# Three-branch attention: VectorE's copy of the turned rows moves one step back, behind the next maximum and the reciprocal

## The reference

```python
def nsa_mixer(q, k_cmp, v_cmp, k_sel, v_sel, k_win, v_win, gate_logit, ...):
    # for each block of 128 queries and each of 16 heads
    p_c = masked_softmax(einsum(q, kc) * scale, cmp_end <= t)      # 31 compressed keys
    o_c = einsum(p_c, vc)
    p_s = masked_softmax(einsum(q, k_g) * scale, valid_s)          # selected blocks
    o_s = einsum(p_s, v_g)
    p_w = masked_softmax(einsum(q, kw) * scale, valid_w)           # window
    o_w = einsum(p_w, vw)
    return gate[0] * o_c + gate[1] * o_s + gate[2] * o_w
```

## Time and profile before

| | |
|---|---|
| time before, median of 3 runs | 1916.68 us (1914.93 to 1918.02) |
| the profiled execution's own time | 1919.38 us |
| its span, first to last instruction | 1917.6 us |
| granted PE clock, mean | 0.988 of full speed |
| PE busy in the span | 1839.3 us (96%) |
| DVE busy | 1027.5 us (54%) |
| ACT busy | 828.2 us (43%) |
| POOL busy | 592.6 us (31%) |
| the three-branch attention, scores to last turn | about 1375 to 1536 us |

### The profile page before, as it was taken

How to read it: one execution, slowest core, us unless ns; L and a number is a source line. 1 busy time by engine, 2 the same in 40 slices (tenths; PEclk the granted TensorE clock), 3 DMA queues, 4 the chain that set the end, 5 groups by cost and what they waited for, 6 DMA issues and landing times.

```text
span 1917.6 us, 27389 instructions
## 1 busy us (share of the span) xinstructions
PE 1839.3 (96%) x10554; PEld 1451.5 (76%) x10554; DVE 1027.5 (54%) x2006; ACT 828.2 (43%) x1569; POOL 592.6 (31%) x421
## 2 busy tenths in 40 slices
PE   8999999997888999999999999999999999999998
PEld 7878889842223778767888888889888888888886
DVE  3170442521111869663477676842577725767677
ACT  4123651311111543375554544353377655444543
POOL 4344431011110233356322223233055643232221
PEclk9999999999999999999999999999999999999999
DMA  7223404699999412121132223222203012233321
GB/s 236 98 94 118 140 1 154 251 392 419 420 420 370 167 45 88 46 88 35 54 132 88 88 88 120 98 94 67 45 2 89 2 44 88 88 131 108 113 88 45
DMA packets 86867, 252.06 MB, mean 131 GB/s; under 512 B 12212, under 2 KB 19700, under 8 KB 74448
## 3 DMA queue, kind: packets, MB, share of 16 engines
q1 hardware_dynamic: 81344, 238.79, 33.9%
q0 software_dynamic: 4592, 9.30, 1.3%
q10 hardware_dynamic: 800, 2.20, 0.3%
HBM read 241.89 MB, written 15.73 MB: 134 GB/s over the span
## 4 chain that ended last, share of the span: by engine, by line
PE 86%; DVE 4%; DMA 4%; ACT 3%; issue 2%; POOL 0%; ACTq 0%; DVEq 0%; POOLq 0%
PE psA L1606 42%; PE psS L2054 4%; PE psA L1649 3%; DMA ring<-in_w_down_e 3%; PE psA L2018 2%; PE psO L2352 2%; PE psO L1836 2%; PE psT L1836 2%; PE psS L1836 2%; PE psT L2402 2%; DVE x L3089 2%; DMA big<-in_w_down_e 1%; PE psA L1471 1%; PE psA L1785 1%; PE psS L1649 1%
## 5 line engine op out<-in xcount | busy, mean ns | idle before, releaser
L1290 POOL TENSOR_TENSOR w_slot<-ring,w_slot 128x1024 fp32r<-128x1024 f32 (+1 forms) x81 | 214.0, 2656 | 524.7 <-ACT w_slot L2433 524.4
L1606 PE MATMUL psA<-hT_hi,w_slot 128*128 128x512 f32 x960 | 298.2, 390 | 0.0
L2433 ACT ACTIVATE w_slot<-ring 128x1024 fp32r<-128x1024 f32 (+2 forms) x183 | 196.8, 1086 | 164.4 <-DVE ring L3089 75.0
L1606 PEld LDWEIGHTS psA<-hT_hi,w_slot 128*128 128x128 f32 x960 | 180.4, 188 | 37.3
L1606 PE MATMUL psA<-hT_lo,w_slot 128*128 128x512 f32 x480 | 187.0, 390 | 0.0
L3089 DVE TENSOR_TENSOR w_slot<-ring,w_slot 128x1024 fp32r<-128x1024 f32 x98 | 119.9, 1225 | 115.7 <-ACT w_slot L2433 115.7
L3089 DVE TENSOR_TENSOR x<-psA,x 128x512 f32<-128x512 f32 (+1 forms) x186 | 117.1, 662 | 104.2 <-PE psA L1606 68.8
L1606 PE MATMUL psA<-w_slot,hid_part 128*128 128x512 f32 x672 | 161.4, 390 | 0.0
L2433 ACT ACTIVATE big<-psA 128x512 f32<-128x512 f32 (+6 forms) x134 | 61.7, 482 | 208.7 <-PE psA L1606 126.0
L1606 PEld LDWEIGHTS psA<-w_slot,hid_part 128*128 128x128 f32 x672 | 126.2, 188 | 26.1
L2433 ACT ACTIVATE scr<-scr,stat 128x384 f32<-128x384 f32 (+3 forms) x224 | 123.7, 555 | 19.1 <-DVE stat L4079 9.8
(11 more groups left out here) (557 smaller groups left out, 4450.2 us busy)
## 6 DMA issues: line engine op xcount, KB each, us to landing
ring<-in_mlp_w SPq DMA_DIRECT2D x32, 2048.0 KB, 8.1
ring<-in_w_in SPq DMA_DIRECT2D x8, 2048.0 KB, 8.1
ring<-in_w_gate_e SPq DMA_DIRECT2D x14, 1024.0 KB, 16.3
ring<-in_w_up_e SPq DMA_DIRECT2D x14, 1024.0 KB, 20.7
ring<-in_w_down_e SPq DMA_DIRECT2D x13, 1024.0 KB, 28.3
big<-in_w_down_e SPq DMA_DIRECT2D x12, 1024.0 KB, 26.4
ring<-in_ab_w_in SPq DMA_DIRECT2D x5, 2048.0 KB, 8.6
scr<-in_w_down_e SPq DMA_DIRECT2D x7, 1024.0 KB, 27.0
```

The lines of the kernel that those rows point to most:

```text
L1290: nc.gpsimd.tensor_tensor(part(w_lo, c), raw_piece(c), part(w_hi, c).bitcast(F32), ALU.subtract)\
L1606: ins = pe.matmul(o, a, b, start=(at == 1), stop=(at == 3 * len(terms)))
L2433: return nc.scalar.activation(o, i, f, **kw)
```

## The change

DVE's loop of the three-branch attention issues the reciprocal or the weighing directly behind the maximum, and the copy behind that; and the copy at step i is that of item i - 7 instead of item i - 6. No instruction is added or removed, and the loops of the other engines are as they were.

```diff
                                 op0=ALU.add, op1=ALU.min, accum_out=negm[:, n_items + i:n_items + i + 1]).then_inc(n_masked, 1)
-                    k = i - TURN_LAG - 1
+                    if 2 <= i < n_nsa + 2 and nsa[i - 2]["g"]:
+                        weigh_nsa(i - 2)
+                    k = i - TURN_LAG - 2
                     if 0 <= k < n_nsa and k % 2:
                         dve.wait_ge(n_turned, k + 1)
                         if k >= TURNED:
                             dve.wait_ge(n_values, values_before(k - TURNED))
                         nc.vector.tensor_copy(turned_probs[k % TURNED][:, 0:nsa[k]["n"]], psT[k % 2][:, 0:nsa[k]["n"]])\
                             .then_inc(n_copied[k % 2], 1)
-                    if 2 <= i < n_nsa + 2 and nsa[i - 2]["g"]:
-                        weigh_nsa(i - 2)
```

## The result

The changed kernel takes 1933.61 us (median of 4 runs, 1933.16 to 1936.64) against 1917.35 us (median of 4, 1914.93 to 1918.14): 16.3 us more, a ratio of 1.009 with a 95% interval of 1.0073 to 1.0108. The forecast was 1929, slower; the time lies in its range, and the loss was about a third larger than the 12.5 us forecast.

A forecast was written before the change was run, and what follows sets the result against it. The prediction took PE to bound the attention, with DVE's later copies stalling its turns: 8.1 us at plain places + 6.7 at weighings - 2.1 given back = 12.7 us, in the runs' measure 1916.7 + 12.5, rounded to 1929 us; range 1920.5 to 1936.

The forecast's parts named there:

- What bounds the attention: Attention: PE sets the pace, busy 146.7 of 152.0 us; a change on DVE counts only where PE waits for it.
- the loop of the psT buffer: Turn of item k, its copy, turn of item k + 2; a maximum now delays the copy, 1.70 us against 1.36 at 384 wide.
- Where it binds: Odd items with no value block before the buffer's next turn: from item 15 on 24 plain places, plus 7 with a weighing.
- The sign that POOL's share of PE's waits would go: Changed kernel's profile: PE's waits for POOL's product, 2.1 us in nine turns before, were to go.
- The price of a plain place: Loops without value block or weighing: stalls of 0.2 to 0.34 us by width, 6.9 us, plus 1.2 for reciprocals: 8.1 us.
- With a weighing: Copies behind the 0.82 us weighing: items 11, 45, 79, 113 cost 3.9 us, items 29, 63, 97 cost 2.8.
- What is given back: PE's nine waits for POOL, 2.1 us, can go as the reciprocal comes earlier; nothing comes back behind the attention.
- The sum: Whole kernel: 8.1 + 6.7 - 2.1 = 12.7 us more, forecast as 1929 us; chance 0.72.
- No change: Rival for the psT loop: two rotating buffers hide one's copy behind the other's turn; 1916.7 us, chance 0.06.
- Faster: Rival: POOL's wait for the reciprocal is the brake in narrow tiles; 5 us less, 1911, chance 0.07.
- Slower by 5 us: Rival: PE is delayed only at the seven weighings, 6.7 us less 2.1; 1921.5 us, chance 0.13.
- The rival of the clock: New stalls in the attention lower PE's granted clock, about 1.7 us per fall, five adding 8; 1937 us, chance 0.02.

The follow-up runs named there:

- dose: Kernel before, with the first 128 columns copied once more ahead of every odd copy, a delay of 0.33 us: 1925.51 us, ratio 1.0033 to 1.0058.
- the halves: Kernel before with reciprocal and weighing ahead of the copy, 1918.23 us; kernel before with only the copy moved to item i - 7, 1930.36 us.
- reciprocal first: Kernel before, with reciprocal and weighing ahead of the copy, which stays that of item i - 6: 1918.23 us, ratio 0.9993 to 1.0012.
- weighing behind: Changed kernel, with the cmp items' weighing behind the copy again and the pairs' reciprocals in front: 1932.94 us, ratio 1.0062 to 1.0089 to before.

## Why the prediction was right, and where it was off

- *What bounds the attention, and the loop of the psT buffer.* Right, and shown from both sides: the copy behind the next maximum costs 14.1 us without the rest of the change, the rest of the change with the copy in front of that maximum costs nothing that the times show, and a measured dose costs itself less the slack at the places worked out ahead.
- *Where it binds.* Right. In the changed kernel the turn that closes the loop starts 0.14 or 0.15 us behind the end of the copy at all 31 places forecast, item 67 among them, which was put at nothing and cost 0.12 us. From item 11 on, three more turns do so that were not counted, those of items 11, 113 and 127 (0.39, 0.24 and 0.26 us); every other one comes at least 0.37 us behind its copy. The list's 29 waits are 28 of the 31 and item 11; at items 81 and 111 it names POOL, and at item 69 the wait is under PEld. Copies delayed only in the other places cost nothing that the times show. The sign that POOL's share of PE's waits would go can't be read from the list, as said above.
- *The price of a plain place.* Too small: 8.1 us forecast, 10.8 measured (the 24 loops from turn to turn, after against before). The step that failed is the 0.04 us between the end of a turn and DVE's maximum. I had read it from a copy. A maximum starts 0.15 us behind the turn (1424.47 against an end at 1424.32), also in the narrow tile (1521.20 against 1521.05). 0.11 us at 31 places are 3.4 us. With it the loop of item 37 is 0.49 + 0.15 + 0.48 + 0.55 + 0.15 = 1.82 us, what was measured. The earlier trace rows start with a copy and could not show it, but the trace of the kernel before does: each of the 14 maxima that a turn released starts 0.14 or 0.15 us behind it. One of them with its turn, and one of the first steps with its scores:

```profile
1444.60 0.60 PE L2402 MATMUL psT<-const,scr 128*128 128x128 f32 x4
...
1445.34 0.69 DVE L4079 CUSTOM_DVE_ANT_0 scr<-psS,const 128x512 f32<-128x512 f32 x1 [1.93 <-PE psT L2402]
```

```profile
1377.43 0.44 PE L2389 MATMUL psS<-nsa_k,nsa_q 128*128 128x128 f32 x2
...
1377.90 0.29 DVE L4079 CUSTOM_DVE_ANT_0 scr<-psS,const 128x128 f32<-128x128 f32 x1 [1.03 <-PE psS L2389]
```

  The second pair says that it is not the instruction itself: in the first seven steps a maximum waits for its scores alone, and the four of them that waited start 0.03 or 0.04 us behind the scores. Nor is it enough that there are two waits: the copies from item 9 on have two as well and start 0.04 us behind the turn. What makes the 0.15 stays open. At items 59, 75 and 83 the period was also shorter than I took it (1.56, 1.56 and 1.47 us, with cmp scores or, at 83, the first 384-wide scores between the turns), and they cost 0.63 to 0.69 us, not 0.27 to 0.36.
- *With a weighing.* 6.7 forecast, 7.9 measured, at the seven items named, 0.92 to 1.33 us each. At item 11 I had taken 0.6 for waits that were there anyway; it cost 1.09.
- *What is given back.* 2.1 forecast. The turns that came earlier did so by 2.0 us in all, at nine turns, mostly where PE had waited for POOL. That is about as forecast, though some of it lies inside the places above.
- *The sum.* In the profiled executions the attention grew by 18.2 us against 12.7: the 31 places cost 18.7 us, not 14.8, and the other loops together gave back 0.5. The medians grew by 16.3.
- *The rivals.* No change falls: the two buffers hide a copy only up to the slack, 0 to 0.33 us, and the rule of the Trainium skill to rotate through PSUM banks ("Perfetto Trace Analysis", section "Optimizing Tensor Performance") holds just to there. Faster falls with the halves: the reciprocals in front bring 0.7 us, and not 5. Slower by 5 us falls: the plain places cost more than the weighings. The rival of the clock falls too: the granted clock of the changed kernel's attention is 1.00, against 0.99 before; what it did is told below.

## What to carry to other kernels

When an instruction is moved back on one engine, find the buffer that it frees and write down the loop through it: producer, hand over, everything that now stands ahead of it on its engine, itself, hand over; and compare that with the time after which the producer comes back. An engine with a quarter of its time idle, as DVE here before the change (busy 112.6 of 152.0 us), can still hold the bound engine up, if its idle time lies in front of the work and not behind it. If two instructions are released by the same event, the one that frees a buffer for the bound engine goes first, and short ones that feed an engine with slack may go ahead of it only while it is waiting anyway.

## What the runs showed of the hardware

After the same stretch of waiting the granted clock of PE fell in some executions and not in others. In the execution of before, PE was busy 2.14 of the 4 us ahead of 1390, and the granted clock of the next four was 0.57, most of that time at the 1.2 GHz level (columns as in the earlier trace rows):

```profile
1386.00:1390.00 4.00, 2.14 (x19) 1.90 (x18) 3.04 (x8) 3.19 (x10) 0.87 (x2) 1.00 0.00 0
1390.00:1394.00 4.00, 4.00 (x24) 3.11 (x22) 2.79 (x11) 2.56 (x9) 0.88 (x2) 0.57 0.00 0
```

In the changed kernel the same work, with the same waits for the query splits, lies 3.0 us earlier in the span. PE was busy as little, and the clock stayed at full speed:

```profile
1383.00:1387.00 4.00, 2.14 (x19) 1.90 (x17) 2.67 (x7) 3.18 (x10) 0.88 (x2) 1.00 0.00 0
1387.00:1391.00 4.00, 4.00 (x31) 2.71 (x29) 2.75 (x10) 2.57 (x9) 0.88 (x2) 1.00 0.00 0
```

From the turn of item 0 to that of item 9 that is 14.46 us before and 13.08 after, 1.4 us that are no effect of the order as far as the others show: of the profiled executions those of before, reciprocal first, weighing behind and dose have a fall here, the other five have none, PE is busy 2.14 us in this stretch in all nine, and both groups hold kernels with either order of the copy. With the 3.0 us by which the attention began earlier, in a part of the program that is the same, it is why the two profiled executions are only 13.8 us apart, and the attention 18.2. What decides the fall was not tested.
